# Delta-rule stage: gate weights through the projection's ring, filler and inversions dealt out anew, weight splits on ScalarE and VectorE

## The reference, cut to what matters

```python
lower = jnp.where(strict, bc[..., :, None] * kk * decay, 0.0)
tinv = lax.linalg.triangular_solve(lower + eye, jnp.broadcast_to(eye, lower.shape),
                                   left_side=True, lower=True, unit_diagonal=True)
u = tinv @ (vc * bc[..., None])
w = tinv @ (kc * (bc * jnp.exp(gc))[..., None])
qk = jnp.einsum('nbhcd,nbhed->nbhce', qc, kc) * decay
def step(state, xs):
    u_i, w_i, qk_i, q_i, k_i, gl_i = xs
    v_new = u_i - w_i @ state
    o_i = q_i @ state + qk_i @ v_new
    state = state * jnp.exp(gl_i)[..., None, None] + jnp.einsum('bhcd,bhce->bhde', k_i, v_new)
    return state, o_i
```

## Time and profile before

| | us |
|---|---|
| median of 3 runs (2808.57 to 2810.16) | 2809.75 |
| the profiled execution | 2812.34 |
| its span, first to last instruction | 2810.6 |
| PE busy in the span | 2573.8 (92%) |
| DVE, ACT, POOL busy | 1066.6, 828.8, 580.3 |
| mean granted TensorE clock | 0.956 |

### The profile page before, as it was taken

One profiled execution on the slowest core, in us unless ns is written; L12 is line 12 of the kernel. 1 busy time (PEld: TensorE's weight loads), 2 busy tenths in 40 slices (PEclk: granted clock), 3 DMA queues, 4 the chain that ended last, 5 costly groups with the idle time before them and its releaser, 6 DMA issues. The chain is left out here.

```text
span 2810.6 us, 33545 instructions
## 1 busy us (share of the span) xinstructions
PE 2573.8 (92%) x12792; PEld 2148.4 (76%) x12792; DVE 1066.6 (38%) x1372; ACT 828.8 (29%) x1261; POOL 580.3 (21%) x497
## 2 busy tenths in 40 slices
PE   6999999797989998997597996999999979999998
PEld 5878888686879886775386785888888768887887
DVE  5665125264535336886643432000000042233332
ACT  4333323251111116775200433112111141233221
POOL 3352247341212110000510322112212100000000
PEclk9999999898999998999598998999999989999999
DMA  4232213575555643222654455322332273345443
GB/s 141 72 91 86 77 53 117 174 249 178 160 174 163 176 127 136 102 107 93 195 168 152 181 172 183 93 75 75 86 82 75 61 244 114 108 153 201 162 147 107
DMA packets 321696, 373.09 MB, mean 133 GB/s; under 512 B 52408, under 2 KB 250168, under 8 KB 316984
## 3 DMA queue, kind: packets, MB, share of 16 engines
q1 hardware_dynamic: 179992, 268.80, 29.7%
q10 hardware_dynamic: 141600, 102.87, 11.9%
HBM read 251.98 MB, written 119.64 MB: 132 GB/s over the span
## 5 line engine op out<-in xcount | busy, mean ns | idle before, releaser
L2304 DVE TENSOR_TENSOR hid_lo<-ff_raw,hid_hi 128x1024 fp32r<-128x1024 f32 x96 | 114.0, 1223 | 837.7 <-ACT hid_hi L2268 837.5
L2214 PE MATMUL y_ps<-w_hi,hid_hi 128*128 128x512 f32 x768 | 301.9, 393 | 29.6 <-DVE w_lo L2298 20.6
L2214 PE MATMUL y_ps<-w_lo,hid_hi 128*128 128x512 f32 x768 | 300.9, 392 | 0.0
L2214 PE MATMUL y_ps<-w_hi,hid_lo 128*128 128x512 f32 x768 | 300.7, 392 | 0.0
L115 PE MATMUL ff_ps<-ffx_hi,w_hi 128*128 128x512 f32 x768 | 216.4, 390 | 16.3 <-DVE ffx_lo L2083 16.3
L115 PE MATMUL ff_ps<-ffx_lo,w_hi 128*128 128x512 f32 x768 | 216.3, 390 | 0.0
L115 PE MATMUL ff_ps<-ffx_hi,w_lo 128*128 128x512 f32 x768 | 215.8, 389 | 0.0
L2268 ACT ACTIVATE hid_hi<-ff_raw 128x1024 fp32r<-128x1024 f32 x96 | 97.4, 1054 | 357.3 <-PE y_ps L2214 329.4
L2214 PEld LDWEIGHTS y_ps<-w_hi,hid_hi 128*128 128x128 f32 x768 | 145.5, 189 | 62.6 <-DVE w_lo L2298 21.9
L115 PEld LDWEIGHTS ff_ps<-ffx_hi,w_hi 128*128 128x128 f32 x768 | 144.4, 188 | 46.6 <-issue 16.7
L115 PE MATMUL proj_ps<-ht_hi,win_hi 128*128 128x512 f32 x576 | 172.8, 408 | 0.0
(11 more groups left out here) (232 smaller groups left out, 4681.2 us busy)
## 6 DMA issues: line engine op xcount, KB each, us to landing
ff_raw<-s_hid_s SPq DMA_DIRECT2D x96, 512.0 KB, 4.4
arena<-s_dn_s SPq DMA_DIRECT2D x24, 1024.0 KB, 5.7
s_hid_s<-ff_stage ACTq DMA_DIRECT2D x32, 768.0 KB, 4.9
w_raw<-in_w_ff_in SPq DMA_DIRECT2D x32, 512.0 KB, 5.9
ff_raw<-in_w_ff_out SPq DMA_DIRECT2D x32, 512.0 KB, 4.9
win_raw<-in_w_in SPq DMA_DIRECT2D x26, 512.0 KB, 3.6
s_made_s<-arena SPq DMA_DIRECT2D x12, 1024.0 KB, 5.7
arena<-s_made_s SPq DMA_DIRECT2D x48, 256.0 KB, 6.3
```

What stands on the lines that cost most here:

```text
L2214: mm = pe.matmul(acc[:, bank(u, t)], x[:, (t if opens(t) else kh), k], y[:, w], start=w == 0 and first == 0, stop=w == KF - 1 and first == 2)
L2304: dve.tensor_tensor(hlo[:, b, ks].rearrange("p k j -> p (k j)"), raw[:, r], f32(hhi[:, b, ks]).rearrange("p k j -> p (k j)"), ALU.subtract ...
```

## The change

It moves the raw, high and low weight buffers out of both stages, so that they are shared: one raw buffer instead of two in the projection and one in the next stage. The projection also loads and splits the first gate tile of the deltanet stage (27 weight tiles, WEIGHTS). In the deltanet stage POOL splits nothing any more: ACT makes the high copy and DVE the low part, each in a `keep_up` at a planned segment (`ready(i)` and the one after), and ACT issues the load of the tile after that. The segments are two waits, twelve makes, four waits, 25 steps, with 24, 22, 24 and 22 fillers. Inversion 0 is cut into three parts that follow makes 8, 9 and 10, inversion 1 has 21 columns ahead of the steps instead of 12, and the woven parts are put into steps 0 to 2 and 5 to 12. SP stores tiles 0 to 10 before the first inverse.

```diff
     WEIGHTS = [col for _, _, col in TILES] + [GATE_COL + EARLY_GATES * P]
...
             def load(n):
-                if n >= 2:
-                    sp.wait_ge(s["w_ready"], n - 1)
-                sp.dma_start(raw[:, n % 2], w_cols[:, :, TILES[n][2]:TILES[n][2] + P]).then_inc(w_in[n % 2], 16)
+                if n:
+                    sp.wait_ge(s["w_ready"], n)
+                sp.dma_start(raw[:], w_cols[:, :, WEIGHTS[n]:WEIGHTS[n] + P]).then_inc(s["w_in"], 16)
...
-            for n in range(2):
-                load(n)
-            with sp.Fori(1, NT // 2) as i:
+            load(0)
+            for u in range(2):
+                load_x(u, 2 + u)
+            load(1)
+            with sp.Fori(2, NT // 2) as i:
...
-            for t, step, n in ((1, copy_hi, 0), (2, subtract_hi, 0), (3, copy_hi, 1), (4, subtract_hi, 1)):
+            for t, step, n in ((1, copy_hi, 0), (2, subtract_hi, 0), (3, None, 0), (4, None, 0), (5, copy_hi, 1), (6, subtract_hi, 1)):
...
-    ORDER = ([("make", t) for t in range(11)] + [("wait", n) for n in range(4)] + [("make", 11)] + [("wait", 4 + n) for n in range(4)] +
+    ORDER = ([("wait", n) for n in range(2)] + [("make", t) for t in range(NT)] + [("wait", 2 + n) for n in range(4)] +
              [("step", v) for v in range(-1, STEPS)])
-    FILL = {"make": 10, "wait": 24, "step": 25}
+    FILL = {"make": 22, "wait": 24, "step": 22}
...
+    def ready(i):
+        return next((seg for seg in range(len(ORDER)) if finished(seg - 1) >= NG * (i - 1)), 0) if i >= 2 else 0
...
-        PRE = 12
+        PRE = 21
         WOVEN = {}
-        for v in range(5):
+        for v in range(3):
             j = PRE + 4 * v
             WOVEN[v] = [(1, j, min(j + 2, BLK - 1)), (1, min(j + 2, BLK - 1), min(j + 4, BLK - 1))]
-        for v in range(6, 14):
-            j = 4 * (v - 6)
+        for v in range(5, 13):
+            j = 4 * (v - 5)
...
@@ SyncE @@
-                for t in range(9):
+                for t in range(NT - 1):
                     if t + 3 < NT:
                         load_feat(t + 3)
                     store_blocks(t)
...
                 load_identity()
-                for t in range(9, NT):
-                    store_blocks(t)
-                    store_made(t)
                 for v in range(2):
                     load_low(v)
+                store_blocks(NT - 1)
+                store_made(NT - 1)
...
-                    if v == 5:
+                    if v == 3:
                         store_inverse(1)
                         load_blocks(2)
                         sp.wait_ge(s["inv_stored"], 128)
                         load_identity()
-                    if v == 14:
+                    if v == 13:
                         store_inverse(2)
...
@@ TensorE @@
                     if kind == "make":
-                        fill(seg, 0.5)
                         if n == 0:
                             sums()
+                        fill(seg, 0.5)
                         make(n)
...
@@ ScalarE, keep_up(seg) behind the sigmoids @@
-                        if g == 1 and i + 2 < len(GATES):
-                            load_weights(i + 2)
-                load_weights(0)
+                    for i in range(1, len(GATES)):
+                        if ready(i) == seg:
+                            act.wait_ge(s["w_in"], 16 * i)
+                            if i >= 2:
+                                act.wait_ge(s["f_done"], NG * (i - 1))
+                            act.activation(whi[:, i % 2], raw[:], ACT.Copy).then_inc(s["w_hi"], 1)
+                        if i > 1 and ready(i - 1) + 2 == seg:
+                            load_weights(i)
+                load_weights(1)
...
-                load_weights(1)
...
@@ VectorE @@
+                def keep_up(seg):
+                    for i in range(1, len(GATES)):
+                        if ready(i) + 1 == seg:
+                            dve.wait_ge(s["w_hi"], i)
+                            dve.tensor_tensor(wlo[:, i % 2], raw[:], f32(whi[:, i % 2]), ALU.subtract).then_inc(s["w_ready"], 1)
...
-                for t in range(9):
-                    make(t)
-                invert(0, 0, BLK - 1)
-                for t in range(9, NT):
-                    make(t)
+                for seg, (kind, n) in enumerate(ORDER):
+                    if kind == "step":
+                        break
+                    keep_up(seg)
+                    if kind == "make":
+                        make(n)
+                        if n in (8, 9, 10):
+                            invert(0, *((0, 11), (11, 21), (21, BLK - 1))[n - 8])
                 invert(1, 0, PRE)
                 for v in range(-1, STEPS):
                     now, after = v >= 0, v + 1 < STEPS
                     if now:
                         make_z(v)
+                    keep_up(SEG["step", v])
                     if after:
                         mask_x32(v + 1)
...
@@ GpSimd @@
-                def split():
-                    i = split_done[0]
-                    pool.wait_ge(s["w_in"], 16 * (i + 1))
...
-                    pool.tensor_copy(whi[:, i % 2], raw[:]).then_inc(s["w_hi"], 1)
-                    pool.wait_ge(s["w_hi"], i + 1)
-                    pool.tensor_tensor(wlo[:, i % 2], raw[:], f32(whi[:, i % 2]), ALU.subtract).then_inc(s["w_ready"], 1)
...
...
 def program(nc, io):
     with ExitStack() as ctx:
         ht_hi, ht_lo = (ctx.enter_context(nc.sbuf_tensor(name, [P, KD, TOK], F32R, align_bytes=512)) for name in ("ht_hi", "ht_lo"))
-        project(nc, io, ht_hi, ht_lo)
-        deltanet(nc, io, ht_hi, ht_lo)
+        raw = ctx.enter_context(nc.sbuf_tensor("win_raw", [P, KD, P], F32, align_bytes=128))
+        whi, wlo = (ctx.enter_context(nc.sbuf_tensor(name, [P, 2, KD, P], F32R, align_bytes=128)) for name in ("win_hi", "win_lo"))
+        project(nc, io, ht_hi, ht_lo, raw, whi, wlo)
+        deltanet(nc, io, ht_hi, ht_lo, raw, whi, wlo)
```

More of the change, by code:

```diff
@@ L142, with project @@
 EARLY_GATES = 3
-def project(nc, io, ht_hi, ht_lo):
+def project(nc, io, ht_hi, ht_lo, raw, whi, wlo):
     SLOT = {"k": 2, "q": 3}
@@ L154, in project @@
     N = len(TILES)
+    WEIGHTS = [col for _, _, col in TILES] + [GATE_COL + EARLY_GATES * P]
     GATING = 14
@@ L212, in project @@
         xps = c.ps("xt_ps", [P, 2, 512])
[L214 to L215 removed]
+        x_in = c.sems2("x_in")
+        names = ("w_in", "const_in", "late_in", "mhalf_done", "passed", "ss_done", "ms_done", "rstd_done", "xn_done", "xt_done", "hi_done", "lo_done",
                  "w_hi", "w_ready", "acc_done", "acc_used", "conv_step", "sig_done", "silu_done", "turn_mm", "turn_used", "sq_done", "reduced", "mean_done", "root_done",
@@ L253, in _ @@
                 load_x(u, u)
-            for n in range(2):
-                load(n)
-            with sp.Fori(1, NT // 2) as i:
+            load(0)
[3 more added lines that the diff above has]
+            with sp.Fori(2, NT // 2) as i:
                 for u in range(2):
                     load_x(u, i * 2 + u)
-            for n in range(2, N):
+            for n in range(2, N + 1):
                 load(n)
@@ L282, in copy_hi @@
             def copy_hi(n):
-                pool.wait_ge(w_in[n % 2], (n // 2 + 1) * 16)
+                pool.wait_ge(s["w_in"], (n + 1) * 16)
                 if n >= 2:
                     pool.wait_ge(s["acc_done"], n - 1)
-                pool.tensor_copy(whi[:, n % 2], raw[:, n % 2]).then_inc(s["w_hi"], 1)
+                pool.tensor_copy(whi[:, n % 2], raw[:]).then_inc(s["w_hi"], 1)
             def subtract_hi(n):
                 pool.wait_ge(s["w_hi"], n + 1)
-                pool.tensor_tensor(wlo[:, n % 2], raw[:, n % 2], f32(whi[:, n % 2]), ALU.subtract).then_inc(s["w_ready"], 1)
+                pool.tensor_tensor(wlo[:, n % 2], raw[:], f32(whi[:, n % 2]), ALU.subtract).then_inc(s["w_ready"], 1)
             def take_root(m):
@@ L348, in _ @@
             root(0, 0)
-            for t, step, n in ((1, copy_hi, 0), (2, subtract_hi, 0), (3, copy_hi, 1), (4, subtract_hi, 1)):
+            for t, step, n in ((1, copy_hi, 0), (2, subtract_hi, 0), (3, None, 0), (4, None, 0), (5, copy_hi, 1), (6, subtract_hi, 1)):
                 root(t % 2, t)
-                step(n)
-            root(1, 5)
-            with pool.Fori(3, NT // 2) as i:
+                if step:
+                    step(n)
+            root(1, 7)
+            with pool.Fori(4, NT // 2) as i:
                 for u in range(2):
@@ L906, with deltanet @@
 BLK = 32
-def deltanet(nc, io, ht_hi, ht_lo):
+def deltanet(nc, io, ht_hi, ht_lo, raw, whi, wlo):
     NB = P // BLK
@@ L943, in deltanet @@
         c = Core(nc, ctx, "deltanet")
-        raw = c.sb("gate_raw", [P, KD, P])
-        whi = c.sb("gate_w_hi", [P, 2, KD, P], F32R)
-        wlo = c.sb("gate_w_lo", [P, 2, KD, P], F32R)
         sig = c.sb("gate_out", [P, 2, 512])
@@ L1589, in clear @@
                     pool.memset(side(inv_in[:, d, 0], d, BLK), 0.0).then_inc(s["cleared"], 1)
```

(5 more changed lines are left out.)

22 lines of the change are left out of this document (6 added, 16 removed).

## The result

| | before | after |
|---|---|---|
| median, us | 2809.75 (2807.05 to 2816.06, 5 runs) | 2820.36 (2819.04 to 2821.51, 5 runs) |
| ratio of after to before | | 1.0034, 95% interval 1.0022 to 1.0046 |
| the profiled execution, its span, clock | 2812.34, 2810.6, 0.956 | 2819.04, 2817.3, 0.957 |

The change makes the kernel slower by 10.6 us, 0.38%.

A forecast was written before the change was run, and what follows sets the result against it. Two chains, TensorE's and the 32x32 inversions', can set the order; the inversions' ends last before step 0. 717.3 + 331.8 + 9.0 = 1058.1 against 1054.1: +4.0, opening -1: +3, so 2813 us, range 2802 to 2823.

The forecast's parts named there:

- likeliest case: Whole kernel: forecast of 2813 us, own range 2808 to 2819, chance 0.50.
- Start: Deltanet stage's opening: TensorE starts at 540.1, stops 4.7 us at filler 48 (6.1 by the skill page), k-k products at 565.4.
- -1: Projection's opening: weight load ahead of tile 4's x and second subtract two roots later give -1 us (-2 to +1.5).
- Rival C: Deltanet stage's start: no stop at filler 48, as ScalarE reaches the sigmoid first; 2807 us, chance 0.07.
- Makes: Makes ahead of the steps: 8.16 us each with 22 fillers instead of 5.44 with 10; tile 7's products at 622.5.
- Inversion chain: Inversions 0 and 1 through memory to step 0's mask end last ahead of the steps; first t32 product at 717.3.
- rival B: Ahead of step 0: inversion chain isn't last, t32 starts about 706, 11.3 us earlier; 2802 us, chance 0.18.
- Steps: First t32 to last step's state products: 331.8 us instead of 356.6, of which 519 instead of 590 fills give -16.1.
- long stop: TensorE's stop in the steps for the stored inverse: 8.2 us instead of 11.1, -2.9 (bounds: none, or -7).
- late z: VectorE's late z in the steps, 3.0 us, both where POOL split weights: -2.8.
- rival A: Steps: VectorE's subtract is late beside POOL's scale and decay; six steps by 1.3 us, +8, 2821 us, chance 0.25.
- Last step: After the last step's state products, no filler left: 9.0 us to the next stage instead of 13.3.

The follow-up runs named there:

- e6: Changed kernel with the sums between the first two wait segments and no TensorE wait for the constants; 2809.29 us, ratio 0.9989 to the kernel before.
- e9: Changed kernel with the identity loaded ahead of both inverse loads and inversion 1 doing 11 columns instead of 21 ahead of the mask; ratio 1.0001 to before.
- e4: Changed kernel with SyncE's wait for inversion 1's stores and the identity load moved behind step 4's inverse load; 2819.02 us, ratio 1.0027 to before.
- e5: Changed kernel with SyncE's inverse loads in the steps put ahead of inverse stores, block loads and the identity; ratio 0.9957 to the kernel before.

## Why the prediction came out as it did

The sign of the sum was right and its size too small. It gave +3 (2813) and called a change within 0.2% likeliest; measured was +10.6, 0.38%. That lies inside the range of 2802 to 2823, but 1.4 us above the 2819 at which the likeliest case's own range ended. The path ahead of step 0 was as forecast; the step that failed is what the stored inverse would cost in the steps.

**Start.** TensorE began at 537.3, not 540.1, since the opening and projection ended 2.8 earlier in this trace. Over twelve traces with the shared ring that end is 1.6 earlier than in the one trace of before: -1 can't be refuted, and one trace of before can't confirm it where twelve lie up to 3.3 apart. From there the sums, the stop (4.7 forecast, 4.5 measured, released by ScalarE) and the first k-k products came as worked out: 24.9 us from first product to k-k, 25.3 forecast. ScalarE's table load and the sigmoid behind it start 1.29 apart (554.87 and 556.16), as in the earlier trace rows, so the stop was not 6.1. Rival C is out, as the stop was there. e6 shows the price of the stop and its clock.

**Makes.** They stand 8.15 us apart (8.16 forecast), and tile 7's products 57.0 after tile 0's (57.1).

**Inversion chain.** From first product to first t32 177.4 us, 177.2 forecast. Its pieces, with the forecast behind each: tile 7 to SyncE's load 7.6 (9.1), landing 10.0 (7.5; the 10.1 of the earlier trace rows was the better guess: with the makes further apart the transfers landed no sooner), inversion 0 with makes 9 and 10 34.0 (34.7), store to identity 19.9 (20.6), its landing 6.3 (5.7), columns and mask 17.7 (17.2). e9 shows that this chain was last; rival B is out (t32 at 714.7 behind a stop for the mask, not at 706). That the sum came out within 0.2 is in part luck: -1.5 and +2.5 nearly cancelled, and the rest with them.

**Steps.** 331.8 forecast, 336.2 measured: the term that failed. "The same SP queue, but the inverse is complete in the first half of its step, 4 us earlier" gave -2.9 for the long stop, and the second was to go with 1.7 of clock. The store went out at 762.20, 5.0 earlier than the 767.16 of before (the two rows below are of before), but the identity behind it went out 17.5 later instead of 15.5, the inverse then landed 11.5 instead of 10.6 later, and TensorE came 2.2 earlier too: 11.1 again. The third inverse's store, moved one step ahead of its reader, was put before another step's load, which landed late instead (2.8).

```profile
767.16 0.55 SPq L1076 DMA_DIRECT2D s_inv_s<-inv_blocks  x1
...
782.71 0.34 SPq L1060 DMA_DIRECT2D inv_blocks<-in_eye_blocks  x1
```

e4 and e5 show what the step left out: the stop was one of SyncE's order, so finishing an inverse sooner only moved it. The late z went as forecast (3.0 to 0.3), and the other terms of the steps, the fills above all, were together 1.3 better than worked out; no run takes them apart.

**VectorE's subtract in the steps.** In the step shown below it took 2.02 us beside POOL's scaling instead of 1.2, and the mask came right behind it, 2.98 after z began instead of the 1.74 of the next step, which has no subtract (765.64 to 767.38), with no stop of TensorE; rival A's mechanism is there, but it stays inside the slack. In after's timelines of VectorE and POOL:

```profile
752.09 1.13 DVE L1497 SCALAR_TENSOR_TENSOR arena<-dn_ps,neg_egc,arena 128x128 f32<-128x128 f32 x4 [0.38 <-PE dn_ps L1181]
753.13 2.02 DVE L1406 TENSOR_TENSOR win_lo<-win_raw,win_hi 128x1024 fp32r<-128x1024 f32 x1
755.07 0.41 DVE L1467 TENSOR_TENSOR arena<-dn_ps,level_masks 128x256 f32<-128x256 f32 x1
...
753.03 1.04 POOL L1579 TENSOR_TENSOR late<-late,g_exps 128x512 f32<-128x512 f32 x1 [4.29 <-PE dn_ps L1181]
...
754.03 2.02 POOL L1573 TENSOR_TENSOR arena<-arena,g_exps 128x512 f32<-128x512 f32 x1
```

**Last step.** From its state products to the next stage's first load 9.5 us (9.0 forecast from pieces that add up to 8.9, 13.3 before).

In sum: the next stage was forecast 4.0 later with no change at the opening. The traces add -2.8 at the start, +0.2 in the chain, +4.4 in the steps and +0.5 at the end: 6.3, where the first load stands 6.2 later. Later stages add 0.4 to 0.5: +6.7, where +3 was forecast. The median moved 3.9 more, which no trace shows. Of the steps' 4.4, the two stops are 5.7 (2.9 and 2.8); the rest of the steps was 1.3 shorter than worked out.

## What to carry to other kernels

A stop whose releaser is a load may come from the order in the issuing engine's list: look which data the load brings, and what was issued or waited for ahead of it, before making the producer faster. A wait for one's own store, and the stores themselves, belong behind the loads that the next step needs. When work moves between engines, list what each engine has queued ahead of it: here the split on VectorE paid 8 to 9 us in the new order, and cost 4 in the old one, behind an inversion of some 24 us in one piece.

## What the runs showed of the hardware

The pair of instructions above resolves how VectorE and POOL exclude each other: POOL's first scaling runs 753.03 to 754.07, VectorE's subtract ends at 755.15, 1.1 after that, and POOL's second ends at 756.05, 0.9 after that; so each seems to run only when the other is done, with that time counted as its own. The Trainium skill (SBUF — State Buffer, SBUF: two separate sides) states such an exclusive lock for the whole instruction; the trace agrees, with 2.02 instead of 1.20 and 2.02 instead of 1.04.

The issue of four 32 KB loads took 1.84 us in one place (after, 780.87) and 9.55 in another (e4, 774.20), with the same 1.5 MB of stores and block loads ahead of them in SyncE's list. In after SyncE had waited for the stores to land, in e4 it had not: its issuing was itself held up while they were under way. In e5 the next four loads behind them (781.67) took 8.1 us to issue, but they were not wanted yet, and TensorE did not stop. What holds it, the transfers' bytes or their small packets, no run tells apart.
